# Seven products instead of eight in a model's four gated up projections, with the weight sums on GpSimd and the modulation sums split between ScalarE and VectorE

## The reference

```python
silu_c = silu(c)
for layer in range(2):
    mod = silu_c @ w_ada[layer] + b_ada[layer]        # 1024 -> 9 * 1024
    sh1, sc1, g1, sh2, sc2, g2, sh3, sc3, g3 = split(mod, 9)
    h = rmsnorm(x, norm_g[layer, 0]) * (1 + sc1) + sh1
    x = x + 0.5 * g1 * ((silu(h @ w1) * (h @ w3)) @ w2)   # D_FF = 2816
    ...                                                # attention mixer, x = x + g2 * ...
    h = rmsnorm(x, norm_g[layer, 2]) * (1 + sc3) + sh3
    x = x + 0.5 * g3 * ((silu(h @ w1) * (h @ w3)) @ w2)   # second pair of weights
```

## Time and profile before

| | |
|---|---|
| runs | 3716.49, 3718.90, 3721.02 us |
| profiled execution, first to last instruction | 3717.0 us (of its own time, only this span is given) |
| TensorE matmuls busy | 3667.4 us, 99% |
| VectorE busy | 1567.6 us, 42% |
| ScalarE busy | 736.1 us, 20% |
| GpSimd busy | 15.9 us |
| DMA | 598.74 MB, mean 161 GB/s |
| chain that ended last | TensorE 98% |

### The profile page before, as it was taken

One profiled execution on the slowest core, in us unless ns is written; L12 is line 12 of the kernel. 1 busy time (PEld: TensorE's weight loads), 2 busy tenths in 40 slices (PEclk: granted clock), 3 DMA queues, 4 the chain that ended last, 5 costly groups with the idle time before them and its releaser, 6 DMA issues.

```text
span 3717.0 us, 42263 instructions
## 1 busy us (share of the span) xinstructions
PE 3667.4 (99%) x18452; PEld 2737.0 (74%) x18452; DVE 1567.6 (42%) x2772; ACT 736.1 (20%) x1434; POOL 15.9 (0%) x43
## 2 busy tenths in 40 slices
PE   6999999999999999999999999999999999999999
PEld 5856697785668687587957679778657977757795
DVE  5434342334420345223833236736523673432384
ACT  1003400100431044211112111133211113521110
POOL 1000000000000000000000000000000000000000
PEclk9999999999999999999999999999999999999999
DMA  9753476554324442343443334432333444334342
GB/s 398 282 199 136 172 293 242 226 196 167 127 104 159 167 150 108 119 159 125 171 159 132 119 114 168 173 140 110 114 115 113 168 173 159 114 113 159 123 178 102
DMA packets 42472, 598.74 MB, mean 161 GB/s; under 512 B 4736, under 2 KB 4752, under 8 KB 6192
## 3 DMA queue, kind: packets, MB, share of 16 engines
q1 hardware_dynamic: 41024, 589.94, 42.9%
q0 software_dynamic: 1264, 6.10, 0.4%
HBM read 594.97 MB, written 1.05 MB: 160 GB/s over the span
## 4 chain that ended last, share of the span: by engine, by line
PE 98%; issue 1%; DVE 1%; ACT 1%; DMA 0%
PE ps L600 25%; PE ps L2602 12%; PE ps L483 9%; PE ps L382 8%; PE ps L463 5%; PE ps L2060 4%; PE ps L503 3%; PE ps L2093 3%; PE ps L796 3%; PE ps L2502 3%; PE ps L1568 2%; PE ps L1588 2%; PE ps L2829 2%; PE ps L1563 2%; PE ps L813 1%; PE ps L625 1%
## 5 line engine op out<-in xcount | busy, mean ns | idle before, releaser
L600 PE MATMUL ps<-hT,ring 128*128 128x256 f32 (+1 forms) x5568 | 941.6, 331 | 3.6 <-DVE stat L324 3.6
L600 PEld LDWEIGHTS ps<-hT,ring 128*128 128x128 f32 x5568 | 855.1, 191 | 88.1 <-issue 7.7
L483 PE MATMUL ps<-ring,aT 128*128 128x512 f32 x784 | 341.1, 592 | 0.0
L483 PEld LDWEIGHTS ps<-ring,aT 128*128 128x128 f32 x784 | 147.9, 190 | 179.1 <-issue 178.9
L463 PE MATMUL ps<-ring,aT 128*128 128x512 f32 x448 | 196.1, 597 | 0.0
L1308 DVE TENSOR_TENSOR aT<-cbuf,ps 128x512 f32<-128x512 f32 x44 | 30.3, 688 | 374.7 <-ACT cbuf L1292 374.7
L223 DVE SCALAR_TENSOR_TENSOR memT<-big,silu_c,memT 128x512 f32<-128x512 f32 x238 | 179.0, 752 | 8.5
L2060 PE MATMUL ps<-hT,ring 128*128 128x256 f32 x768 | 174.5, 384 | 0.0
L525 ACT ACTIVATE big<-x 128x1024 f32<-128x1024 f32 x34 | 35.9, 1057 | 696.6 <-DVE x L577 389.9
L2060 PEld LDWEIGHTS ps<-hT,ring 128*128 128x128 f32 x768 | 146.8, 193 | 26.7 <-issue 7.7
L463 PEld LDWEIGHTS ps<-ring,aT 128*128 128x128 f32 x448 | 85.1, 191 | 103.6 <-issue 103.5
(11 more groups left out here) (546 smaller groups left out, 4634.9 us busy)
## 6 DMA issues: line engine op xcount, KB each, us to landing
ring<-weights_in SPq DMA_DIRECT2D x244, 2048.0 KB, 7.7
big<-ada_in SPq DMA_DIRECT2D x34, 2048.0 KB, 7.8
ring<-ada_in SPq DMA_DIRECT2D x2, 2048.0 KB, 22.7
big<-b_gate_in POOLq DMA_DIRECT2D x1, 1536.0 KB, 17.3
x<-x_in SPq DMA_DIRECT2D x1, 1024.0 KB, 4.8
big<-b_gate_in POOLq DMA_DIRECT2D x1, 1024.0 KB, 8.9
big<-mem_in POOLq DMA_DIRECT2D x1, 1024.0 KB, 5.5
out<-big SPq DMA_DIRECT2D x2, 512.0 KB, 2.6
```

The source lines that it names most:

```text
L483: last = pe.matmul(ps[:, 2 * t + half, :], aT[:, 4 * c + k, t * P:(t + 1) * P], w[:, k, half * 512:(half + 1) * 512], start=first, stop=(4 ...
L600: last = pe.matmul(ps[:, bank + m // 2, (m % 2) * SEQ + at:(m % 2) * SEQ + at + n], w[:, k, m * P:(m + 1) * P], hT[:, k, at:at + n], start ...
```

## The change

What it does, in five parts:

1. In the four gated stages, chunks 2 to 10 are done by seven block products (`up_pe`), in the same scheme as the convolution-gated stages. The seven results are combined by seven VectorE instructions of 128x256 (`up_out_dve`), ScalarE first copies the first product and later applies Silu, VectorE multiplies from SBUF.
2. The four weight sums of each of these chunks are GpSimd instructions (`up_left_pool`), one set of s1, s2, s4 in SBUF for all chunks, so s1 of a chunk waits for the third product of the chunk before, s2 for its fifth, s4 for its last. The four token sums are made once for each stage on VectorE (`up_right_dve`).
3. A slice is scaled in place by ScalarE, eight instructions of 128x512 with silu_c[:, k] as scale (`ada_scale_act`), and summed by VectorE in one reduction of 128x512 out of 128x4096, whose input runs over k innermost, in steps of 512 elements (`ada_sum_dve`).
4. The order around slices changes: in a gated stage VectorE's turn of chunk j is: combine, take slice j-1, sum slice j+1, multiply; TensorE reduces slice j-1 in the middle of chunk j. The last slice of stage one is reduced behind the first down chunk, which waits for the stage's last multiplication.
5. GpSimd's DMAs are moved around the new calls; the memory's normalisation in the fourth gated stage moves from chunks 2 to 5 to the stage's start; semaphores are renamed and recounted.

```diff
+        def ada_scale_act(act, a):
+            act.wait_ge(ada_loaded[a if a < 4 else a % 2], 16 if a < 4 else 16 * (a // 2))
+            w = ada_slot(a)
+            for k in range(KT):
+                last = act.activation(w[:, k, :], w[:, k, :], ACT.Copy, scale=silu_c[:, k:k + 1])
+            last.then_inc(ada_scaled, 1)

         def ada_sum_dve(dve, a):
             if a >= 2:
                 dve.wait_ge(ada_reduced, a - 1)
-            dve.wait_ge(ada_loaded[a if a < 4 else a % 2], 16 if a < 4 else 16 * (a // 2))
-            w = ada_slot(a)
-            dve.tensor_scalar(ada_sum[:, a % 2, :], w[:, 0, :], silu_c[:, 0:1], None, ALU.mult).then_inc(ada_step, 1)
-            for k in range(1, KT):
-                dve.wait_ge(ada_step, 8 * a + k)
-                dve.scalar_tensor_tensor(out=ada_sum[:, a % 2, :], in0=w[:, k, :], scalar=silu_c[:, k:k + 1], in1=ada_sum[:, a % 2, :], op0=ALU.mult, op1=ALU.add).then_inc(ada_step, 1)
+            dve.wait_ge(ada_scaled, a + 1)
+            dve.tensor_reduce(ada_sum[:, a % 2, :], ada_slot(a).rearrange("p k c -> p c k"), AX.X, ALU.add).then_inc(ada_step, 1)

+        def up_left_pool(pool, n, i, c0):
+            s1, s2, s4 = (up_left_part(part) for part in range(3))
+            up_ready(pool, i)
+            for j in range(2, 11):
+                w = arrived(pool, c0 + j).rearrange("p (k c) -> p k c", k=KT)
+                a11, a12, a21, a22 = w[:, 0:4, 0:SEQ], w[:, 4:8, 0:SEQ], w[:, 0:4, SEQ:512], w[:, 4:8, SEQ:512]
+                if j > 2:
+                    pool.wait_ge(gated_products, up_products_count(n, j - 1, 2))
+                pool.tensor_tensor(s1, a21, a22, ALU.add).then_inc(gated_left, 1)
+                pool.wait_ge(gated_left, up_left_count(n, j, 1))
+                pool.tensor_tensor(a21, a11, a21, ALU.subtract).then_inc(gated_left, 1)
+                if j > 2:
+                    pool.wait_ge(gated_products, up_products_count(n, j - 1, 3))
+                pool.tensor_tensor(s2, s1, a11, ALU.subtract).then_inc(gated_left, 1)
+                if j > 2:
+                    pool.wait_ge(chunks_used, c0 + j)
+                pool.wait_ge(gated_left, up_left_count(n, j, 3))
+                pool.tensor_tensor(s4, a12, s2, ALU.subtract).then_inc(gated_left, 1)

+        def up_pe(pe, n, c0, j, ada, mem):
...
+            if j >= 4:
+                pe.wait_ge(gated_out, up_out_count(n, j - 2, 5))
+            elif j == 2:
+                pe.wait_ge(swiglu_dve_done, 11 * n + 1)
+            product(1, w[:, 4:8, 0:SEQ], hT[:, 4:8, 0:P])
+            product(0, w[:, 0:4, 0:SEQ], hT[:, 0:4, 0:P]).then_inc(gated_products, 1)
+            pe.wait_ge(seven_tokens, up_right_count(n) + 4)
+            pe.wait_ge(gated_left, up_left_count(n, j, 1))
+            product(2, s1, t1).then_inc(gated_products, 1)
+            if j == 2:
+                pe.wait_ge(swiglu_dve_done, 11 * n + 2)
+            product(4, w[:, 4:8, SEQ:512], t4)
+            for a in ada:
+                ada_reduce_pe(pe, a, up_ada_place(j), taken=0)
+            pe.wait_ge(gated_left, up_left_count(n, j, 3))
+            product(3, s2, t2).then_inc(gated_products, 1)
+            if j > 2:
+                pe.wait_ge(gated_out, up_out_count(n, j - 1, 4))
...
+            product(6, w[:, 0:4, SEQ:512], t3)
+            pe.wait_ge(gated_left, up_left_count(n, j, 4))
+            product(5, s4, hT[:, 4:8, P:SEQ]).then_inc(chunks_used, 1)

+        def up_out_dve(dve, n, c0, j):
...
+            dve.wait_ge(chunks_used, c0 + j + 1)
+            dve.wait_ge(swiglu_act_done, up_act_count(n, j, 1))
+            dve.tensor_tensor(part, gate[:, :, 0:P], p6, ALU.add).then_inc(gated_out, 1)
+            dve.tensor_tensor(gate[:, :, 0:P], gate[:, :, 0:P], p2, ALU.add)
...
+            dve.tensor_tensor(late, part, p5, ALU.add).then_inc(gated_out, 1)
...
+            dve.tensor_tensor(gate[:, :, P:SEQ], late, p3, ALU.add).then_inc(gated_out, 1)
+            dve.tensor_tensor(part, part, p7, ALU.add).then_inc(gated_out, 1)
...
+            dve.tensor_tensor(up[:, :, P:SEQ], part, p5, ALU.add)
+            dve.tensor_tensor(up[:, :, 0:P], part, p4, ALU.add).then_inc(gated_out, 1)

         def swiglu_act(act, n, c0, ada=(), mem=False):
...
+                if j >= 2:
+                    act.wait_ge(gated_products, up_products_count(n, j, 1))
+                    act.wait_ge(swiglu_dve_done, 11 * n + j - 1)
+                    act.copy(gate[:, :, 0:P], up_block(j, 0).rearrange("p (m c) -> p m c", m=2)).then_inc(swiglu_act_done, 1)
+                    act.wait_ge(gated_out, up_out_count(n, j, 3))
+                    act.activation(gate, gate, ACT.Silu).then_inc(swiglu_act_done, 1)
...
+                for a in ada[j + 1:j + 2]:
+                    ada_scale_act(act, a)

         def swiglu_dve(dve, n, i, c0, ada=(), mem=False, seven=None):
...
+                if j >= 2:
+                    up_out_dve(dve, n, c0, j)
+                    for a in ada[j - 1:j]:
+                        ada_take_dve(dve, a, up_ada_place(j))
+                    for a in ada[j + 1:j + 2]:
+                        ada_sum_dve(dve, a)
+                dve.wait_ge(swiglu_act_done, up_act_count(n, j, 1 if j < 2 else 2))
...
+                dve.tensor_tensor(aT[:, 2 * j:2 * j + 2, :], cbuf[:, j % 2, 0:2, 4:260], up, ALU.mult).then_inc(swiglu_dve_done, 1)

         def down_pe(...):
...
                 if j < len(ada):
-                    ada_reduce_pe(pe, ada[j], 6 + ada[j] % 2)
+                    if j == 0:
+                        pe.wait_ge(*then)
+                    ada_reduce_pe(pe, ada[j], ada_bank(6 + ada[j] % 2))

         def _(pool):
             start_pool(pool, 0, None)
             attn_pool(pool, 0)
+            up_left_pool(pool, 0, None, c0=0)
+            attn_pool(pool, 1)
             gates_pool(pool, 0)
-            attn_pool(pool, 1)
+            up_left_pool(pool, 1, 1, c0=26)
             gates_pool(pool, 1)
+            up_left_pool(pool, 2, 2, c0=43)
             mem_pool(pool)
             mamba_pool(pool, (attn_dve_done, 4), layer=0)
+            up_left_pool(pool, 3, 4, c0=69)
```

More of the change, by code:

```diff
@@ L286, in norm_act @@
             act.activation(silu_c[:, :], column('c', 0, KT), ACT.Silu).then_inc(start_act_done, 1)
+            act.wait_ge(start_act_done, 1)
+            for a in range(4):
+                ada_scale_act(act, a)
             act.wait_ge(norm_pe_done, 2)
@@ new lines, in up_act_count, with up_right_count, up_out_count, up_ready @@
+        def up_act_count(n, j, step):
+            return 20 * n + (j if j < 2 else 2 * j - 2) + step
+        def up_right_count(n):
+            return (0, 4, 8, 21)[n]
+        def up_out_count(n, j, step):
+            return 45 * n + 5 * (j - 2) + step
+        def up_ready(engine, i):
+            if i is None:
+                engine.wait_ge(norm_act_done, 5)
+                engine.wait_ge(norm_dve_done, 7)
+            else:
+                engine.wait_ge(down_act_done, 6 * i + 6)
+                engine.wait_ge(down_dve_done, 8 * i + 8)
@@ new lines, in up_pe, with product @@
+        def up_pe(pe, n, c0, j, ada, mem):
+            w = arrived(pe, c0 + j).rearrange("p (k c) -> p k c", k=KT)
+            s1, s2, s4 = (up_left_part(part) for part in range(3))
+            t1, t2, t3, t4 = (up_right_part(part) for part in range(4))
+            def product(place, left, right):
+                for m in range(2):
+                    for k in range(4):
+                        last = pe.matmul(up_block(j, place)[:, m * P:(m + 1) * P], left[:, k, m * P:(m + 1) * P], right[:, k, :], start=(k == 0), stop=(k == 3), skip_group_check=True)
+                return last
+            if j >= 4:
[10 more added lines that the diff above has]
+            product(4, w[:, 4:8, SEQ:512], t4)
+            for a in ada:
+                ada_reduce_pe(pe, a, up_ada_place(j), taken=0)
[3 more added lines that the diff above has]
+                pe.wait_ge(gated_out, up_out_count(n, j - 1, 4))
+            elif mem:
+                pe.wait_ge(mem_act_done, 4)
+                pe.wait_ge(mem_dve_done, 4)
+            product(6, w[:, 0:4, SEQ:512], t3)
+            pe.wait_ge(gated_left, up_left_count(n, j, 4))
+            product(5, s4, hT[:, 4:8, P:SEQ]).then_inc(chunks_used, 1)
@@ L3073, in _ @@
             swiglu_pe(pe, 3, 4, c0=69, mem=True)
-            down_pe(pe, 5, (swiglu_dve_done, 43), c0=80, nk=22, then=(swiglu_dve_done, 44), seven=1, taken=(swiglu_act_done, 44))
+            down_pe(pe, 5, (swiglu_dve_done, 43), c0=80, nk=22, then=(swiglu_dve_done, 44), seven=1, taken=(gated_out, up_out_count(3, 10, 5)))
             mamba_pe(pe, 0, 5, c0=86)
@@ L3098, in _ @@
             convglu_pe(pe, 3, 16, c0=227, w_col=COL['f_conv_w_2'] + 198, b_col=COL['f_conv_b_2'] + 66)
-            last_pe(pe, (convglu_dve_done, 172), c0=238, then=(gated_out, 220), seven=5, taken=(gated_out, 220))
```

(1 more changed line is left out.)

201 lines of the change are left out of this document (121 added, 80 removed).

## The result

Before, 3719.42 us (median of 6 runs, 3716.49 to 3721.56); after, **3732.06 us** (median of 6, 3729.68 to 3734.87). The ratio is **1.0037**, 95% interval 1.0026 to 1.0048. The forecast was 3707 us and faster: its sign was wrong, though the time lies in its range. The profiled span is 3733.2 us; it belongs to the longest of the six runs (3734.87), 2.8 us above the median.

What follows compares the result with a forecast made beforehand. TensorE, busy 99% of 3717.0 us, was taken as the bound: 3717.0 - 47.1 (fewer products) + 35.4 (slices) = 3705.3, plus 1.9 to the runs' median, 3707 us, 0.3% faster; range 3670 to 3750.

Steps and rivals of the forecast that it cites:

- TensorE's gain: Nine chunks in each of four gated stages fall from 13.815 to 12.506 us each, 47.1 us in all.
- The reduction: VectorE's strided sum of one slice, called R: 7.1 us, ends 4.4 and 7.8; loop hidden while under 5.6.
- 24 R - 135: Slices' total cost for reduction time R above 6.6 us: 16 loops, four loops less 4.1, four starting reductions; 35.4 forecast.
- the plain-rate rival: Slice reduction unslowed by its stride takes 4.4 us, loop 12.2 stays hidden, all 47.1 arrive: 3672 us; chance 0.19.
- The one-source case at full rate: Skill's one-source operation alternating between two regions at full rate; by it the slice reduction takes 4.4, total 3672 us.
- The start: Before the first chunk: scaling, then four slice reductions ending at 45.4 instead of 35.9, so 9.5 us later.
- The loop's members: ScalarE-VectorE slice turn: combining 1.66, Silu 0.60, scalings 4.8, reduction 7.1, multiply 0.69, signals 0.05; 14.9 against TensorE's 13.4.
- In my timing the multiply falls mostly into GpSimd's pause: Gated chunks: VectorE's multiply mostly falls before GpSimd's next s1, so their exclusion over SBUF was given no cost.
- The rival that had this mechanism: GpSimd becomes the bound: a multiply waiting for a whole sum adds up to 2.5 to 16 loops, 3747 us; chance 0.10.
- The down projection waits for chunk 9's multiply.: End of stages one and two: wait ends with eight loops each 1.5 us over TensorE's turn, 12.0 us a stage.
- The granted clock is 1.00 in all of them, so it is no term here.: TensorE's clock in the profiled windows of gated stages, with and without slices, is full; no cost was given.
- theory A: Follow-up tests' theory: scaling, reduction and combination in one turn eat the gain; the products alone should give 3672 us.

Runs made afterwards that it cites:

- the combined kernel: Kernel after with first four slices summed as before, scaling one turn ahead from fifth slice, multiply before reduction, no taken-slice wait: 3673.26 us, ratio 0.9875.
- ahead: Kernel after with each slice scaled one turn earlier and VectorE multiplying before it reduces the next slice: 3704.81 us, ratio 0.9963.
- contiguous: Kernel after with the reduction reading eight neighbouring numbers instead of eight lying 512 apart, so sums are wrong: 3681.66 us, ratio 0.9902.
- the 8 products: Kernel after with 8 more unused TensorE products of 128x512 ahead of each of the first two down projections: 3727.61 us, ratio 1.0026.
- the slices alone: Kernel before with only the slices changed (eight ScalarE scalings, one VectorE reduction), products as before: 3744.67 us, ratio 1.0077.
- The products alone: Kernel after with the slices summed as before by eight VectorE instructions, no scaling on ScalarE: 3728.64 us, ratio 1.0027.
- tiny sums: GpSimd's four sums cut to one element each, waits kept: on the products alone 3679.39 us (0.9897), on the kernel after 3722.95 us (1.0017).

## Why the prediction was wrong

**Right.** TensorE's gain: 36 x 1.31 = 47.1 us (the fourth stage gave its 11.8, the combined kernel 46.0 of the 47.1). The reduction: 7.1 forecast, 7.31 measured, in its forecast's own range; at that price the formula 24 R - 135 costs 5.0 us more. That it came so close is partly luck: 7.1 is the middle of two rows of other operations. The lower, 4096 x 1.48 ns + 0.15, is 6.2 and not 6.3; the upper, 7.8, takes four transpositions with their fixed part four times, and with 0.15 us of it once it would have been an estimate of 7.4. The stride: 4.42 without, as the plain-rate rival had it; the Vector Engine (DVE) Microarchitecture Reference of the Trainium skill (Measured stream behaviour on trn2) gave 1.73 ns an element for one source that hops each time, and the runs give 7314/4096 = 1.79. The one-source case at full rate, of which the forecast also told, is not what this reduction did. The start: 9.5 forecast, 9.9 in the trace, 9.5 on the clock when undone. GpSimd's sums at 2.5 and never the bound: 2.39. The loop's members and its place in stages one and two: turns of 15.06 where nothing held them, forecast 14.9. (s4 is needed 10.7 us into its chunk, after six products, not 8.9; this only adds room.)

**Wrong, in three steps, each of which said "nothing".**

1. *"In my timing the multiply falls mostly into GpSimd's pause"*, and the cost of nothing for the sums beside VectorE. Undone, this is worth 9.1 us by the medians. The multiply was mostly in the pause, in fact (median 0.693 us; its 36 cases have 6.6 us too much between them); but line 272 (10.7 too much), the token sums in the second and third stage (up to 2.86 instead of 0.69) and a scaling at 583.53 (line 263, 2.52 instead of 0.43, just before TensorE's longest wait inside a stage, 3.59) were not counted. In a loop that is already late, a hold inside the turn is on the path. The rival that had this mechanism took a whole sum for all 16 loops and 40 us; the size was off, not the mechanism.

2. *"The down projection waits for chunk 9's multiply."* It waits for a slice taken in chunk 10's turn, a combination later: 221.27 instead of 218.19. Undone, 5.0 us. The wait was there before and cost nothing, as the slice had been taken at 197.76, 7 us ahead of the down projection. Now the slice is taken behind the combination of chunk 10, which needs that chunk's last product, so TensorE waits 2.9 and 3.1 us even where VectorE is not late (`ahead`, `contiguous`). The call's argument names chunk 9's multiply; the line under the wait for it names the slice.

3. *"The granted clock is 1.00 in all of them, so it is no term here."* It was 1.00 in stages in which TensorE never waited. The long waits ahead of the down projections cost a second time in slow products: 3.1 and 2.9 us in the two first down chunks, shown by the 8 products (4.5 us net). Inside the stages the slow products mostly lie beside VectorE's lateness: in the first stage of the kernel after, VectorE's combinations behind them (158.41, 203.62) start without waiting for TensorE; in the second one waits 0.50 us (595.77). In the slices alone, where VectorE was not late, they did cost: 3 of the second stage's 9.0 us.

By the medians the forecast missed 24.3 us: it had 11.7 less than before, and 12.6 more came (the table's 27.9 goes by the longest of the six runs and has the 1.6 of the attention stretch in it). The three undone one by one give 18.6 us, the reduction's excess by the formula 5.0: 23.6 together. By the ratios the three give 16.0, and 21.0 together. The remainder of 1 to 3 us was not isolated, and is within what the rounds differ by; the steps were not shown to be additive. The combined run hides the reduction's length and the holds by its order and does not split them.

I also had the reason for the change's two halves wrong while testing: theory A took the slices for the cause and the products for innocent. The products alone, at +10 us and at -37 with tiny sums, show that GpSimd's sums cost 48 to 49 us with the slices as they were.

## What to carry to other kernels

Work given to GpSimd is not beside VectorE's if both read SBUF twice: before moving it, list VectorE's instructions with two SBUF operands, down to the smallest, and its scalings from SBUF to SBUF, and allow each that may fall beside a GpSimd instruction that instruction's length; feed them from PSUM or use a reduction instead. When a change brings waits to an engine that had none, price the wait and the slower clock behind it, and look at every wait on the path that was free before. And a loop over three engines can be shortened by its order: one turn of look-ahead and a multiply moved ahead of a reduction gave 27 us here with the right sums. The faster reduction gave 50, but only with wrong ones; made right by the layout, it moved its stride to ScalarE and the turn became longer.

## What the runs showed of the hardware that I had not expected

- VectorE instructions with two SBUF inputs alternate with GpSimd's, whole instruction by whole instruction, down to the smallest: 4 numbers a partition (line 272) took up to 2.26 us beside sums of 2.4. A scaling with one SBUF input and one SBUF output (line 220 in the products alone, 0.48 us otherwise) took up to 2.57 us there too, so one input isn't always safe; the same section of the Trainium skill says so of a scaling that uses both ports. The reduction was never held (at most 7.41 us).
- After waits of 2.9 and 3.1 us the first 32 records of a down projection took 15.43 to 16.92 us in different runs, after 7.8 us 17.0 (full clock 13.90). A wait of 1.5 us behind 7 us of products left it at 13.97, but one of 1.47 us inside the first stage (191.96) was followed by a granted clock of 0.68 over 3.6 us. The length of the wait alone does not tell.
- ScalarE is slowed by a stride as VectorE is: 512 numbers eight apart, read and written, took 1.232 us on average instead of 0.709; the reduction over numbers 512 apart 7.31 us instead of 4.42.
- One f32 product of 128x512 is two records and takes 0.86 us; I had counted a record as a product, and so added twice the intended work.
